# TensorE starts three chunks of an output unit before the mixer's sums of squares, and VectorE centres before the third low part

## The reference

```python
y_a = rmsnorm(b_a * conv_out_a, out_norm_a_g)
z = jax.nn.silu(layernorm(conv_out_b + conv_b_b.astype(glu.dtype), conv_norm_g, conv_norm_b))
y_b = rmsnorm(z, out_norm_b_g)
y = jnp.einsum('ble,ed->bld', jnp.concatenate([y_a, y_b], axis=-1), w_out)
```

## Time and profile before

| | |
|---|---|
| median of three runs | 1481.31 us (1479.9 to 1481.33) |
| profiled execution | 1481.05 us |
| its span | 1479.3 us, 25091 instructions |
| TensorE matmul busy | 1446.6 us (98%) |
| VectorE busy | 1240.4 us (84%) |
| GpSimd busy | 885.9 us (60%) |
| ScalarE busy | 629.1 us (43%) |
| mean granted TensorE clock | 0.996 of full speed |

### The profile page before, as it was taken

One profiled execution on the slowest core, in us unless ns is written; L12 is line 12 of the kernel. 1 busy time (PEld: TensorE's weight loads), 2 busy tenths in 40 slices (PEclk: granted clock), 3 DMA queues, 4 the chain that ended last, 5 costly groups with the idle time before them and its releaser, 6 DMA issues.

```text
span 1479.3 us, 25091 instructions
## 1 busy us (share of the span) xinstructions
PE 1446.6 (98%) x8568; PEld 1323.9 (90%) x8568; DVE 1240.4 (84%) x2516; ACT 629.1 (43%) x845; POOL 885.9 (60%) x552
## 2 busy tenths in 40 slices
PE   6998989999999999999999999999999999999997
PEld 6998989999999999999999999888888888888886
DVE  7999884799999999677788852799999999999985
ACT  6334543233333333466666754333333333333332
POOL 4687433557688888766766776355555555555500
PEclk9999999999999999999999999999999999999999
DMA  4222313748699999879999999999999999999961
GB/s 178 100 71 71 104 43 108 248 145 304 200 331 325 340 326 339 298 274 367 366 366 355 374 359 410 358 369 387 380 406 386 401 387 394 375 408 385 380 229 69
DMA packets 120259, 433.35 MB, mean 293 GB/s; under 512 B 12384, under 2 KB 12640, under 8 KB 118528
## 3 DMA queue, kind: packets, MB, share of 16 engines
q1 hardware_dynamic: 62592, 212.88, 40.2%
q0 software_dynamic: 46080, 167.79, 30.0%
q10 hardware_dynamic: 11520, 51.93, 8.7%
HBM read 379.34 MB, written 52.69 MB: 292 GB/s over the span
## 4 chain that ended last, share of the span: by engine, by line
PE 82%; DMA 1%; DVE 1%; issue 1%; POOL 0%; ACT 0%; DVEq 0%; ACTq 0%; SPq 0%
PE ps_unit L845 34%; PE ps_misc L914 24%; PE ps_unit L914 12%; PE ps_unit L820 6%; PE ps_misc L880 3%; PE ps_misc L785 1%; DMA gates_even<-gates_dram 1%; PE ps_misc L789 0%; POOL w_lo L513 0%; PE ps_unit L772 0%; PE ps_misc L910 0%; DVE rows L1705 0%; DVE gate_parts L1594 0%; DVE gate L1547 0%; PE ps_unit L910 0%
## 5 line engine op out<-in xcount | busy, mean ns | idle before, releaser
L513 POOL TENSOR_TENSOR w_lo<-raw,w_hi 128x1024 fp32r<-128x1024 f32 x172 | 416.3, 2422 | 209.7 <-issue 128.9
L577 POOL DMA_INDIRECT rows<-v_rows,expert x160 | 258.8, 1617 | 234.6 <-DVE sums L1459 161.2
L845 PE MATMUL ps_unit<-mov_hi,w_hi 128*128 128x384 f32 x1024 | 351.6, 343 | 1.6 <-POOL w_lo L513 1.6
L845 PE MATMUL ps_unit<-mov_lo,w_hi 128*128 128x384 f32 x1024 | 345.1, 337 | 0.0
L845 PE MATMUL ps_unit<-mov_hi,w_lo 128*128 128x384 f32 x1024 | 344.5, 336 | 0.0
L960 ACT ACTIVATE w_hi<-raw 128x1024 fp32r<-128x1024 f32 x300 | 315.4, 1052 | 47.4 <-ACT act_ring L1133 33.7
L1449 DVE CUSTOM_DVE_ANT_0 rows<-rows,ps_unit 128x1024 f32<-128x1024 f32 x160 | 190.4, 1213 | 29.4 <-DMA rows<-u_rows,expert 29.0
L1177 ACT ACTIVATE prod_hi<-prod 128x384 fp32r<-128x384 f32 x128 | 67.3, 526 | 335.5 <-PE ps_unit L914 329.8
L845 PEld LDWEIGHTS ps_unit<-mov_hi,w_hi 128*128 128x128 f32 x1024 | 192.4, 188 | 2.1 <-ACT w_hi L960 1.9
L845 PEld LDWEIGHTS ps_unit<-mov_lo,w_hi 128*128 128x128 f32 x1024 | 192.5, 188 | 0.0
L845 PEld LDWEIGHTS ps_unit<-mov_hi,w_lo 128*128 128x128 f32 x1024 | 192.2, 188 | 0.0
(11 more groups left out here) (255 smaller groups left out, 2561.9 us busy)
## 6 DMA issues: line engine op xcount, KB each, us to landing
raw<-stream SPq DMA_DIRECT2D x300, 512.0 KB, 6.0
acts_dram<-act_ring ACTq DMA_DIRECT2D x64, 384.0 KB
gates_dram<-gates ACTq DMA_DIRECT2D x12, 2048.0 KB, 10.9
acts_in<-acts_dram SPq DMA_DIRECT2D x32, 768.0 KB, 8.7
gates_even<-gates_dram SPq DMA_DIRECT2D x12, 1024.0 KB, 13.1
gates_odd<-gates_dram SPq DMA_DIRECT2D x12, 1024.0 KB, 13.1
rows<-u_rows,expert POOLq DMA_INDIRECT x160, 7.0
rows<-v_rows,expert POOLq DMA_INDIRECT x160, 8.4
```

The costliest lines, as they stand in the source:

```text
L513: nc.gpsimd.tensor_tensor(w_lo[:, j, :], raw[:, j, :], w_hi[:, j, :].bitcast(F32), ALU.subtract).then_inc(lo_made, 1)
L577: nc.gpsimd.indirect_dma_start(out=rows[:, n % ROWS_RING, :], out_offset=None, in_=table, in_offset=bass.IndirectOffsetOnAxis(ap=expert[:, ...
L845: last = nc.tensor.matmul(dense_psum(j), w[:, j, k * P:(k + 1) * P], m[:, k, 0:DENSE], start=(k == 0 and n == 0), stop=(k == KC - 1 and n ...
```

## The change

`out_unit` gets two arguments: the chunks to work on, and whether it closes (signals the end). The first output unit is called twice. The first call comes right behind the sums for the mean, with chunks 0 to 2 of both halves and without a signal; it takes over the wait for ScalarE's last copy of the input projection. The second call has only the last chunk, and stands where the whole unit stood, behind the sums of squares. On VectorE the low part of the third chunk moves behind the four centrings.

```diff
--- before.py
+++ after.py
@@ -694,7 +694,7 @@
                     unit(lap, j, mov_hi, mov_lo)
 
 
-            def out_unit(group, n):
+            def out_unit(group, n, chunks=range(WC), closing=True):
                 j = n % RING
                 ready = KC + group * WC if n == 0 else None
                 u = FIRST_OUT + group * WC + n
@@ -702,12 +702,14 @@
                 pe.wait_ge(lo_made, u + 1)
                 for o in range(2):
                     q = KC * group + 2 * n + o
+                    if not closing and o == 0:
+                        pe.wait_ge(act_took, N_IN)
                     if q in (2, 3):
                         pe.wait_ge(std_made, 5 - q)
                     elif q > 3:
                         pe.wait_ge(dve_took, q - 3 if q < 6 else q - 1)
                     out = out_psum(q)
-                    for k in range(WC):
+                    for k in chunks:
                         if ready and o == 0:
                             pe.wait_ge(mov_hi_made, ready + k + 1)
                             pe.wait_ge(mov_lo_made, ready + k + 1)
@@ -717,16 +719,17 @@
                                 last = nc.tensor.matmul(out[:, a, :], w[:, j, at:at + P],
                                                         mov[:, WC * group + k, a * HALF:(a + 1) * HALF],
                                                         start=(k == 0 and m == 0), stop=(k == WC - 1 and m == 2))
-                    last.then_inc(unit_done if o else out_half_done, 1)
+                    if closing:
+                        last.then_inc(unit_done if o else out_half_done, 1)
 
             pe.wait_ge(conv_b_made, WC)
             channel_sum(lambda c: proj[:, 2 * c], range(WC), WC, 0)
+            out_unit(0, 0, range(WC - 1), closing=False)
             channel_sum(lambda c: sq[:, c], range(WC), WC, 1, SQ_X + WC - 1)
             pe.wait_ge(a_added, 1)
             pe.wait_ge(sq_made, SQ_X + 2 * WC)
             channel_sum(lambda n: sq[:, (WC, KC - 1)[n]], range(2), 2, 0)
-            pe.wait_ge(act_took, N_IN)
-            out_unit(0, 0)
+            out_unit(0, 0, (WC - 1,))
             out_unit(0, 1)
             out_unit(0, 2)
             pe.wait_ge(dve_took, WC)
@@ -1329,13 +1332,16 @@
                                              proj[:, 2 * c + 1, T_PROMPT:T], ALU.mult))
                 settle()
                 conv_b(c)
-            for c in range(WC - 1):
+            def low_a(c):
                 mov_low(KC + c, c, proj[:, 2 * WC + 3 * c], par_col("out_a_g", c))
 
+            low_a(0)
+            low_a(1)
             dve.wait_ge(sum_done, 2)
             for c in range(WC):
                 nc.vector.scalar_tensor_tensor(out=halves(proj[:, 2 * c]), in0=sum_psum(0), scalar=-1.0 / WIDTH,
                                                in1=halves(proj[:, 2 * c]), op0=ALU.mult, op1=ALU.add).then_inc(centred, 1)
+            low_a(2)
             for c in range(1, WC - 1):
                 dve.wait_ge(sq_made, SQ_X + c + 1)
                 ins = nc.vector.tensor_tensor(sq[:, WC], sq[:, WC], sq[:, WC + c], ALU.add)
```

## The result

| | before | with the change |
|---|---|---|
| median of 11 runs | 1481.33 us (1479.9 to 1485.72) | 1485.56 us (1483.27 to 1488.9) |
| profiled execution, its span | 1481.05, 1479.3 us | 1484.89, 1483.1 us |

The ratio is 1.0025 (95% interval 1.0015 to 1.0034): slower, by 3.7 us (2.2 to 5.0) by the ratio; the medians lie 4.2 us apart. A second set of 9 runs of the same kernel, beside other runs of before, gave 1.0027 (1.0017 to 1.0037).

The account below looks back on a forecast made before the run. The prediction took the end of TensorE's sums of squares, which sets the root, as the bound: 1481.05 + 3.37 = 1484.42 us, plus 0.26 to the median, gave 1484.7 us; range 1482.3 to 1487.2.

Parts of the forecast that it names:

- The order on VectorE: VectorE centrings first, squares 1.70 us earlier; third low part issued at 144.65, after GpSimd's multiplication, ending at 145.56.
- rival B: GpSimd's weight split runs before the third low part, holding it until about 147.60: +5.4 us, 1486.7 us; chance 0.13.
- The order on TensorE: Third early chunk waits for its low part until 145.70, TensorE idle 2.61 us, 24 products queued ahead of the sums.
- Rival C: Sums of squares not held by the third early chunk; root 3.5 us earlier, 1477.8 us; chance 0.07.
- The clock in the gap: TensorE's clock falls around the 2.61 us idle, 145.72 to 149.14: root +3.37 us, against +1.64 without the fall.
- rival A: Clock stays at 2.4 GHz through TensorE's gap before the third early chunk: +1.64, 1482.9 us; chance 0.22.
- rival D: Second clock fall, from 2.95 us of TensorE idle ahead of the fifth half unit: another 1.7 us, 1486.4; chance 0.18.

Follow-up runs that it names:

- e1: The change with VectorE's old order back (third low part ahead of the centring), TensorE's three early chunks kept; ratio to before 1.0003.
- e4: The change with its 36 early products chunk by chunk, both output halves of a chunk before the next; ratio to before 1.0006.
- e6: The change with two chunks early instead of three and cache copies moved ahead of VectorE's first low part; ratio to before 0.9992.
- e3: The change plus 18 products with unused results between the second and third early chunk, filling TensorE's gap; ratio to before 1.0014.
- e2: The change's VectorE order alone, with TensorE doing the whole first output unit behind the sums of squares as before; ratio to before 0.9990.
- e7: e2 with the cache copies moved into VectorE's idle ahead of the first low part; ratio to before 0.9986.
- e8: e6 with VectorE's second reciprocal moved ahead of the four scalings; ratio to before 0.9991.

## Why the prediction was right

*The order on VectorE.* Predicted from t0 (prediction's time less 137.59): third low part issued at 7.06, ended at 7.97. Measured 7.06 and 7.06 + 0.91 = 7.97. Reading GpSimd's queue instruction by instruction gave this; rival B, with the split first, did not come, on the margin of 0.33 us as worked out (144.39 less 144.05 is 0.34).

*The order on TensorE.* Predicted: third chunk at 8.11, sums at 12.85, root at 16.72, second unit at 21.90, fifth half unit at 30.87. Measured: 8.12, 12.73, 16.60, 21.79, 30.70. So +3.20 instead of +3.37, and e1 and e4 show the cause by taking it away in two ways; e6 leaves out the late chunk and does so too. Rival C fell: the sums stayed behind the waiting chunk, as the row of 2.37 us shows.

*The clock in the gap.* It fell, as I took it, and the size that I gave it is about right: e3 gives back 1.51 of my 3.37 - 1.64 = 1.73. But my reason, that 2.61 us is nearer to 2.83 than to 2.21, was weak: the wait of 2.21 us ahead of the turn, after which the clock stayed up in the earlier trace rows, is there with the same length in the change and is followed by 1.2 GHz. The length of the wait before a fall does not settle it. The Trainium skill, "TensorE: Matmul & The Clock Gate", section "HAM oscillation — how this bites in real kernels", lays the fall to longer gaps than any of these; the runs do not agree with it, and rival A fell.

*What I left out.* A fall of the clock from 159.58, behind the wait of 1.89 us, made the second unit longer; it cost nothing, since the fifth half unit waits for VectorE anyway (1.13 us instead of the 2.95 predicted). That is also why rival D did not come in the change: the idle that it needed was filled by the slow unit. And the 1.45 us behind the turn of the gates were not in the sum at all, nor the 0.60 us that the start gave. 3.20 + 1.45 - 0.60 - 0.20 (the -0.02 and -0.18 of the result) = 3.85: that 3.37 stands so near to the difference of the profiled executions is partly luck.

*What stays open.* Why the clock falls behind the turn of the gates in five of the ten profiles (the change twice, e1, e3, e6) and not in the others, at the same wait of 2.21 us (2.67 in e4). It is not explained by the low part's place (e1 has the fall, e2 and e7 have not), nor by the wait's length (e4 waits 2.67 us there and keeps the clock). No run was made to settle it. The runs on record show that executions of one kernel differ: those of before timed beside the experiments have a mean granted clock of 0.992 to 0.996 and took 1479.86 to 1485.47 us; every one above 1484.5 us had 0.992 or 0.993. So the 1.45 us belong to the two profiled executions, and are not shown to come of the change. The 3.20 us stand apart from this: among runs with a mean clock of 0.995, the 19 of before took 1480.28 to 1482.70 us and the 6 of the change 1483.98 to 1485.74.

## What to carry to other kernels

Before work is pulled forward into an idle stretch of an in-order engine, look at the last input that any of it needs, and at what is queued behind that wait: here a chunk whose input had itself been moved back stood ahead of the one result that set the path. Put first what is ready (e6), or as much of it as possible between the waits (e4); either took the loss away, though neither was clearly faster than before. And where a change brings an engine's work forward, ask whom the earlier work meets: e2's root was 3 us earlier and its reciprocal 2.8 us later.

## What the runs showed of the hardware

- A VectorE copy of 8 elements per partition, SBUF to SBUF, took 2.36 us beside a weight split on GpSimd, against 0.17 free (e2). Instructions with two SBUF inputs were held likewise: an addition of squares took 1.99 us against 0.72 for the one behind it (before), a low part 1.78 against 0.78 (before), four scalings 4.21 against 2.56 (e6, e8). Reciprocals (3.55 us beside the splits in e7 and e8, and elsewhere) and centrings from PSUM (2.60 us for four beside GpSimd, before and with the change) were not. The Trainium skill, "GPSIMD Engine Reference", section "8. Key points", names instructions with two SBUF inputs and those in a two-port mode as the ones that contend with GpSimd. The additions agree with the first part; whether the copies ran in such a mode no run here shows.
- A fall of the clock behind the turn of the gates costs 1.4 to 1.6 us (10.59 to 10.74 against 9.16 to 9.18 us), as much as half of the effect under study, and comes in some executions of a kernel only. Starting points counted from a common event, as t0 here, keep such falls apart from what the order costs; at +-0.1% the medians alone do not.
